# A gather kernel with its query weights loaded once: new release times for the gather buffers, a longer lag and a moved work list

## The chip, the cores and the metric

The kernel runs on one core of a Trainium2 chip. The metric is the device time of one execution in microseconds, lower is better. It was timed three times before the change; the profile is one further execution. A run of this kernel repeats within a few microseconds.

## The reference, cut to what matters

One layer of an encoder on 512 tokens of width 1024, all in float32. A modulated LayerNorm, one input projection, two kinds of attention (8 neighbourhood heads, 4 differential heads), an output projection and a second LayerNorm come first. The second half, which takes most of the time, is a retrieval over 16384 experts, each with one down row and one up row of 1024 numbers:

```python
qc = (xc @ w_query).reshape(CHUNK, HEADS, 2, DKEY // 2)          # 8 heads
s_half = einsum('chpk,pnk->chpn', qc, sub_keys)                  # 2 x 128 key scores
top_s, top_i = top_k(s_half, 16)                                 # then top 16 of the 16 x 16 sums
expert, g = ..., softmax(best_s)
act = gelu(einsum('chkd,cd->chk', expert_down[expert], xc))
out = einsum('chkd,chk->cd', expert_up[expert], g * act)
```

The output is a LayerNorm of the residual and this sum.

## The kernel before, in words

The 512 tokens are 4 tiles of 128. A **head** is here one token tile with one retrieval head: 32 heads, in the order (tiles 0 and 1, retrieval heads 0 to 3), (tiles 0 and 1, 4 to 7), then tiles 2 and 3 likewise. Each head chooses 16 experts for each of its 128 tokens. A **set** is one of these 16 choices: 512 sets. For every set GpSimd issues two indirect DMAs (L623), each of 128 rows of 4 KB: the **down gather** and the **up gather**.

- The down gather is reduced by VectorE: one instruction multiplies it with the tokens and sums the row (L1379, "the dot").
- After four dots ScalarE takes the Gelu (L889), VectorE multiplies in the softmax weight (L1336, `weigh`), ScalarE spreads four weights on diagonal matrices (L1026), and TensorE adds weight times up gather to the tile's sum (L837).
- A gathered block lies in a **place** until its dot or its matmuls are done. `PLACES` is 8. Places are given out in the order of the gathers, the one used longest ago first; a gather waits for the last use of its place. `LATE_PLACES` adds four places each time a weight buffer has been used for the last time: by query weights of chunk 0 for tile 1 (new places from about set 62 of the down gathers), chunk 1 for tiles 2 and 3 (269), and chunk 2 (305). `PLACE_SETS` is how many sets after that use the places may be asked for.
- `gather_order` writes out the order of the 1024 gathers on GpSimd's queue: down gather `at`, then up gather `at - UP_LAG` (7). Gathers are counted here from 0 in this order; set 0's up gather is gather 8.

The retrieval starts before the first half has ended. `FIRST_GROUPS` are TensorE's pieces of work (groups) before the first up matmul. What is left of it is listed in `SCHEDULE` as (first slot, pieces per slot, groups): after the up matmuls of set `at` TensorE does the pieces of slot `at`. A group is an output projection half (`out`, 8 pieces, L691), a transposition (`mix_t` L681, `u_t` L673), 128 query columns (`query`, 8 pieces, L665), or key scores (L699). Each group writes a PSUM bank; `bank_at` gives it, and `wait_for_bank` lets the first piece wait until the group before in the same bank has been read. Groups in `FIRST_GROUPS` use bank `(g + 3) % 6` after the attention, groups behind them bank `4 + g % 2`.

ScalarE reads query, key score and transposition groups (`evacuate`), in line with its diagonals: a group ended at slot s is read after the diagonal of set s + `EVAC_AFTER` (3). VectorE reads `out` groups in `add_mix`, after the dot named by `ADD_AT`. After the dots named by `LN_FROM` it does eight steps of LayerNorm of token tile 1, 2 and 3; steps 2 and 6 wait for a square root on ScalarE (`ln_deviation`, L875). In the first 8 sets of each head it also chooses the experts of the head after it (`choose`, two steps per set). `residual` (L1347 and on) and `finish` close a token tile after head 12 (tile 0), 16, 28 and at the end.

SyncE loads weights. The 512 columns of query chunk 0 and chunk 1 are loaded during the first half, chunk 2 and 3 over the buffers of the output projection after its last use. In the kernel before, chunk 1's buffer is given to places 8 to 11, and chunk 1 is loaded a second time (2 MB, into chunk 0's buffer) after chunk 0's last use.

Of the kernel before, what the change touches and what calls it, by code (L numbers as in the profile page):

```python
# [72 lines left out]
LATE_PLACES = [(0, ("query", (1, 3, 1, 1))), (1, ("query", (1, 3, 2, 2))), (2, ("query", (2, 3, 2, 2)))]  # L73
PLACE_SETS = 16
QUARTER = 4
UP_LAG = QUARTER + 3
FIRST_UP = UP_LAG
# [21 lines left out]
def query_slot(c, first):  # L99

    return QUERY_SLOT[0] if c == 1 and first >= 2 else QUERY_SLOT[c]


# [11 lines left out]
CHOOSE_FIRST = {31 + i: (i // 8, 2 * (i % 8)) for i in range(16)}  # L115


def phase_a_groups():
# [9 lines left out]
    for a in range(len(ATT) + 3):  # L128
# [4 lines left out]
        if a >= 3:  # L133
# [3 lines left out]
    g += [("query", (1, b, 0, 1)) for b in range(4)] + [("key_scores", (1, 0))]  # L137
# [21 lines left out]
EVAC_AFTER = 3
# [108 lines left out]
def build(nc, x, c, w_ada, b_ada, w_in, w_out, na_rpb, t5_bias, lambda_q1, lambda_k1, lambda_q2,  # L268
# [3 lines left out]
    with ctx:  # L272
# [180 lines left out]
        def _(sp):  # L453
# [75 lines left out]
            def load_query(c, slot, last_use):  # L529

                sp.wait_ge(pe_group, INDEX[last_use] + 1)
                sp.dma_start(w_slot[slot], w_query[0, :, c * HALF:(c + 1) * HALF]
                             .rearrange("(k p) n -> p k n", p=P)).then_inc(w_in_slot[slot], 16)

            load_query(2, QUERY_SLOT[2], ("out", (TILES - 1, 0)))
            load_query(3, QUERY_SLOT[3], ("out", (TILES - 1, 1)))
# [3 lines left out]
            load_query(1, query_slot(1, 2), ("query", (0, 3, 2, 2)))  # L540
# [88 lines left out]
        def _(pe):  # L629
# [31 lines left out]
            def query_part(ps, c, b, first, n, k):  # L661
# [3 lines left out]
                return nc.tensor.matmul(ps[:, 0:n * P], w_slot[query_slot(c, first)][:, k, b * P:(b + 1) * P],  # L665
# [197 lines left out]
        def _(act):  # L863
# [155 lines left out]
            def diagonals(head, q):  # L1019

                act.wait_ge(weight_done, head * QUARTER + q + 1)
                for j in range(q * QUARTER, (q + 1) * QUARTER):
# [5 lines left out]
                    for group in ended_at(at - EVAC_AFTER):  # L1028
# [443 lines left out]
```

## Time and profile before

| | us |
|---|---|
| median of 3 runs | 1754.54 (1750.51 to 1756.98) |
| profiled execution, its own time | 1758.13 |
| its span, first to last instruction | 1756.3 |
| TensorE, VectorE, ScalarE, GpSimd busy | 1479.7, 1140.1, 432.3, 985.6 |
| DMA traffic | 606.02 MB, mean 345 GB/s |

Busy time is a sum over very different stages. The span has two: the first half up to about 380 us, bound by the engines, and the gathers after it. The rows of the slices and windows show how fast data moved in each; a slice is 43.9 us.

### The profile page before, as it was taken

What the parts mean: (1) busy time and instruction counts of PE and PEld (TensorE: products, weight loads), DVE (VectorE), ACT (ScalarE), POOL (GpSimd) and SP (SyncE); (2) the same over time, 40 slices, a digit from 0 to 9 for tenths busy, and PEclk for the clock granted to TensorE, in tenths of its full rate; (3) what the DMA queues carried; (4) which work ended last, traced back from release to release, by engine and by line L of the source; (5) the groups of instructions that cost most, each with busy time, mean ns of one, the idle gap of its engine ahead of it and who ended that gap; (6) DMA issues with size and microseconds to landing.
All of it is one profiled execution on the core that took longest, in us unless ns stands there. A gap on an engine that the chain in (4) does not pass through costs nothing.

```text
span 1756.3 us, 14526 instructions
## 1 busy us (share of the span) xinstructions
PE 1479.7 (84%) x4096; PEld 684.0 (39%) x4096; DVE 1140.1 (65%) x2797; ACT 432.3 (25%) x1096; POOL 985.6 (56%) x1055
## 2 busy tenths in 40 slices
PE   5999989879899989977798799987899777777776
PEld 5444455654454345422343344432344222222222
DVE  6543055777867657776767666776666766677753
ACT  2111142441322222222222222322222222222221
POOL 1000000036767757777776677777777777777771
PEclk9899997989999999999999999999999999999999
DMA  9869221069999999999999999999999999999993
GB/s 308 326 224 218 96 72 21 7 242 374 390 388 409 406 366 391 409 409 409 409 409 408 408 409 409 410 410 409 410 409 409 409 409 409 410 409 409 410 409 152
DMA packets 190679, 606.02 MB, mean 345 GB/s; under 512 B 30704, under 2 KB 31112, under 8 KB 190440
## 3 DMA queue, kind: packets, MB, share of 16 engines
q0 software_dynamic: 147456, 536.94, 77.1%
q1 hardware_dynamic: 41799, 64.29, 11.3%
q10 hardware_dynamic: 1344, 3.87, 0.8%
q8 instruction: 34, 0.56, 0.1%
q14 instruction: 46, 0.37, 0.1%
HBM read 601.68 MB, written 3.34 MB: 344 GB/s over the span
## 4 chain that ended last, share of the span: by engine, by line
DMA 40%; PE 27%; POOL 14%; DVE 11%; issue 7%; ACT 1%; SPq 0%; DVEq 0%; POOLq 0%; ACTq 0%
DMA big<-in_expert_down,expert_idx 14%; DMA big<-in_expert_up,expert_idx 13%; PE pair L633 12%; POOL big L623 11%; PE pair L837 9%; DMA region_v<-in_expert_down,expert_idx 6%; DMA region_v<-in_expert_up,expert_idx 6%; POOL region_v L623 3%; PE pair L691 3%; DVE big L1379 3%; DVE big L1212 1%; DMA big<-in_w_ada 1%; PE pair L665 1%; PE pair L785 1%; DVE region_v L1379 1%
## 5 line engine op out<-in xcount | busy, mean ns | idle before, releaser
L837 PE MATMUL pair<-big 128*128 128x512 f32 x1460 | 710.1, 610 | 159.7 <-DMA big<-in_expert_up,expert_idx 147.0
L1379 DVE CUSTOM_DVE_ANT_0 big<-big,pair 128x1024 f32<-128x1024 f32 x363 | 442.6, 1220 | 250.1 <-DMA big<-in_expert_down,expert_idx 245.7
L837 PEld LDWEIGHTS pair<-big 128*128 128x128 f32 x1460 | 252.0, 190 | 547.3 <-issue 502.7
L623 POOL DMA_INDIRECT big<-in_expert_down,expert_idx x363 | 344.3, 948 | 150.1 <-issue 91.8
L623 POOL DMA_INDIRECT big<-in_expert_up,expert_idx x365 | 348.4, 955 | 127.1 <-issue 79.5
L837 PE MATMUL pair<-region_v,big 128*128 128x512 f32 x588 | 284.2, 606 | 61.6 <-DMA region_v<-in_expert_up,expert_idx 58.6
L1379 DVE CUSTOM_DVE_ANT_0 region_v<-region_v,pair 128x1024 f32<-128x1024 f32 x149 | 181.5, 1220 | 100.3 <-DMA region_v<-in_expert_down,expert_idx 97.7
L1026 ACT ACTIVATE big<-ident,big 128x128 f32<-128x128 f32 x512 | 167.1, 391 | 311.2 <-DVE big L1336 311.2
L633 PE MATMUL pair<-big 128*128 128x512 f32 (+1 forms) x480 | 194.2, 599 | 0.0
L837 PEld LDWEIGHTS pair<-region_v,big 128*128 128x128 f32 x588 | 101.8, 190 | 208.1 <-issue 187.9
L582 POOL TENSOR_SCALAR small<-small 128x4 f32<-128x4 f32 (+1 forms) x6 | 1.4, 236 | 318.6 <-DVE small L1308 282.1
L623 POOL DMA_INDIRECT region_v<-in_expert_down,expert_idx x149 | 141.3, 948 | 62.9 <-issue 38.3
L623 POOL DMA_INDIRECT region_v<-in_expert_up,expert_idx x147 | 139.4, 948 | 55.3 <-issue 30.2
L889 ACT ACTIVATE big<-big 128x4 f32<-128x4 f32 x128 | 26.1, 204 | 505.5 <-DVE big L1379 505.5
L665 PE MATMUL pair<-big 128*128 128x256 f32 (+1 forms) x640 | 141.2, 338 | 0.8 <-ACT big L925 0.8
L665 PEld LDWEIGHTS pair<-big 128*128 128x128 f32 x640 | 104.6, 191 | 86.7 <-issue 85.1
L633 PEld LDWEIGHTS pair<-big 128*128 128x128 f32 (+1 forms) x480 | 84.3, 196 | 93.3 <-issue 91.7
L925 ACT ACTIVATE big<-pair 128x512 f32<-128x512 f32 (+2 forms) x74 | 33.5, 457 | 214.0 <-PE pair L665 107.8
L691 PE MATMUL pair<-big 128*128 128x512 f32 x128 | 65.0, 620 | 0.7 <-issue 0.7
L1212 DVE SCALAR_TENSOR_TENSOR big<-big,small 128x512 f32<-128x512 f32 x84 | 63.2, 752 | 3.0
L1003 ACT ACTIVATE big<-pair 128x512 f32<-128x512 f32 (+3 forms) x70 | 37.6, 540 | 109.9 <-PE pair L633 99.7
L944 ACT ACTIVATE big<-big,small 128x256 f32<-128x256 f32 (+1 forms) x64 | 39.1, 610 | 78.3 <-DVE small L1284 78.3
(148 smaller groups left out, 1029.4 us busy)
## 6 DMA issues: line engine op xcount, KB each, us to landing
big<-in_w_ada SPq DMA_DIRECT2D x12, 2048.0 KB, 18.2
big<-in_w_in SPq DMA_DIRECT2D x6, 2048.0 KB, 17.0
big<-in_w_query SPq DMA_DIRECT2D x5, 2048.0 KB, 18.9
big<-in_expert_up,expert_idx POOLq DMA_INDIRECT x365, 15.5
big<-in_expert_down,expert_idx POOLq DMA_INDIRECT x363, 15.3
big<-in_w_out SPq DMA_DIRECT2D x2, 2048.0 KB, 10.3
big<-na_scr SPq DMA_DIRECT2D x24, 128.0 KB, 5.0
region_v<-in_expert_down,expert_idx POOLq DMA_INDIRECT x149, 13.0
```

The lines of the kernel that those rows point to most:

```text
L623: nc.gpsimd.indirect_dma_start(places[place], None, (expert_down if kind == "down" else expert_up)[0], bass.IndirectOffsetOnAxis(expert_id ...
L633: last = nc.tensor.matmul(ps, a, b, start=(i == 0), stop=(i == len(pairs) - 1))
L665: return nc.tensor.matmul(ps[:, 0:n * P], w_slot[query_slot(c, first)][:, k, b * P:(b + 1) * P], src, start=(k == 0), stop=(k == KB - 1))
L691: return nc.tensor.matmul(ps[:, :], src, w_slot[OUT_SLOT[s]][:, k, :], start=(k == 0), stop=(k == KB - 1))
L837: last = nc.tensor.matmul(pair[t % 2][:, s * HALF:(s + 1) * HALF], diag[:, j, :], places[place][:, s * HALF:(s + 1) * HALF], start=(h == 0 ...
L889: nc.scalar.activation(acts[:, head % 2, lo:lo + QUARTER], at_head(dots, head)[:, lo:lo + QUARTER], ACT.Gelu).then_inc(gelu_done, 1)
L925: nc.scalar.activation(dst, ps, ACT.Copy).then_inc(act_evac, 1)
L944: nc.scalar.activation(exps, raw, ACT.Exp, bias=row_min[:, slot:slot + 1], scale=-1.0, accum_out=row_sum[:, slot:slot + 1]).then_inc(exp_d ...
L1003: nc.scalar.activation(dst, ps, ACT.Copy, scale=scale).then_inc(act_evac, 1)
L1026: nc.scalar.activation(diag[:, j, :], ident[:, :], ACT.Copy, scale=weights[:, head % 2, j:j + 1]).then_inc(diag_done, 1)
L1212: last = v.scalar_tensor_tensor(out=acc, in0=w[:, k, :], scalar=c_exp[:, k:k + 1], in1=acc, op0=ALU.mult, op1=ALU.add)
L1379: v.tensor_tensor_reduce(out=places[place], in0=places[place], in1=u_cur[:, :], scale=1.0, scalar=0.0, op0=ALU.mult, op1=ALU.add, accum_ou ...
```

## The change

Chunk 1 is loaded once: `query_slot` goes, and the second load on SyncE's queue with it. Chunk 1's buffer is therefore busy until slot 245, and the first four late places come from chunk 0's buffer instead. With `PLACE_SETS` 20 the places are 8 until down set 229, 12 until 265, 16 until 301 and 20 from there. The lag between down and up gathers is 10 for sets below 140 and 7 from there (at sets 140 to 142 two up gathers follow each down gather). Group reads on ScalarE move to s + lag - 2. `out (1, 0)` moves from slots 0 to 7 into `FIRST_GROUPS`, as group 229 of what are now 230, and most of the schedule moves ahead by some slots. LayerNorm of tiles 1, 2 and 3 starts at sets 24, 142 and 152, where it started at 25, 92 and 168.

```diff
 PLACES = 8
-LATE_PLACES = [(0, ("query", (1, 3, 1, 1))), (1, ("query", (1, 3, 2, 2))), (2, ("query", (2, 3, 2, 2)))]
-PLACE_SETS = 16
+LATE_PLACES = [(1, ("query", (0, 3, 2, 2))), (0, ("query", (1, 3, 2, 2))), (2, ("query", (2, 3, 2, 2)))]
+PLACE_SETS = 20
-FIRST_UP = UP_LAG
+LONG_LAG, LONG_UNTIL = 10, 140
...
-CHOOSE_FIRST = {31 + i: (i // 8, 2 * (i % 8)) for i in range(16)}
+CHOOSE_FIRST = {32 + i: (i // 8, 2 * (i % 8)) for i in range(16)}
...
-    g += [("query", (1, b, 0, 1)) for b in range(4)] + [("key_scores", (1, 0))]
+    g += [("query", (1, b, 0, 1)) for b in range(4)] + [("key_scores", (1, 0)), ("out", (1, 0))]
...
-SCHEDULE = [(0, 1, [("out", (1, s)) for s in range(2)]), (18, 1, [("mix_t", (2, s)) for s in range(2)]),
-            (26, 4, [("u_t", (1, s)) for s in range(2)]),
-            (28, 4, [("query", (0, b, 1, 1)) for b in range(4)]), (38, 1, [("key_scores", (0, 1))]),
-            (39, 4, [("query", (1, b, 1, 1)) for b in range(4)]), (49, 1, [("key_scores", (1, 1))]),
-            (50, 2, [("out", (2, s)) for s in range(2)]),
-            (60, 1, [("mix_t", (3, 0))]), (63, 1, [("mix_t", (3, 1))]), (66, 1, [("out", (3, s)) for s in range(2)]),
-            (85, 2, [("query", (2, b, 0, 2)) for b in range(4)]), (103, 1, [("key_scores", (2, t)) for t in range(2)]),
-            (105, 2, [("query", (3, b, 0, 2)) for b in range(4)]), (123, 1, [("key_scores", (3, t)) for t in range(2)]),
+SCHEDULE = [(0, 1, [("out", (1, 1))]), (20, 1, [("mix_t", (2, s)) for s in range(2)]),
+            (22, 4, [("u_t", (1, s)) for s in range(2)]),
+            (24, 4, [("query", (0, b, 1, 1)) for b in range(4)]), (34, 1, [("key_scores", (0, 1))]),
+            (35, 4, [("query", (1, b, 1, 1)) for b in range(4)]), (45, 1, [("key_scores", (1, 1))]),
+            (46, 2, [("out", (2, s)) for s in range(2)]),
+            (56, 1, [("mix_t", (3, 0))]), (59, 1, [("mix_t", (3, 1))]), (62, 1, [("out", (3, s)) for s in range(2)]),
+            (80, 2, [("query", (2, b, 0, 2)) for b in range(4)]), (98, 1, [("key_scores", (2, t)) for t in range(2)]),
+            (100, 1, [("query", (3, b, 0, 2)) for b in range(4)]), (133, 1, [("key_scores", (3, t)) for t in range(2)]),
...
-LN_FROM = {1: 25, 2: 92, 3: 168}
-ADD_AT = {15: (1, 0), 23: (1, 1), 62: (2, 0), 67: (2, 1), 82: (3, 0), 90: (3, 1)}
+LN_FROM = {1: 24, 2: 142, 3: 152}
+ADD_AT = {14: (1, 0), 23: (1, 1), 63: (2, 0), 68: (2, 1), 84: (3, 0), 92: (3, 1)}
-WEIGHED = [max(QUARTER * (n + 1), 2 * QUARTER) for n in range(HEADS * QUARTER - 1)]
+WEIGHED = [max(QUARTER * (n + 1), LONG_LAG + n) for n in range(HEADS * QUARTER - 1)]
...
+def lag_at(at):
+    return LONG_LAG if at < LONG_UNTIL else UP_LAG
+
+def evacuated_at(at):
+    return [g for slot in range(max(0, at - LONG_LAG), at + 1) if slot + lag_at(slot) - 2 == at
+            for g in ended_at(slot)]
...
-            if at >= FIRST_UP and ups <= at - UP_LAG:
+            if ups <= at - lag_at(at):
...
-            load_query(1, query_slot(1, 2), ("query", (0, 3, 2, 2)))
...
-                    for group in ended_at(at - EVAC_AFTER):
+                    for group in evacuated_at(at):
```

## Rows read from the trace of the kernel before

**Rows 1.** The page's slices of 43.9 us: data moved, GB/s.
```profile
GB/s 308 326 224 218 96 72 21 7 242 374 390 388 409 406 366 391 409 409 409 409 409 408 408 409 409 410 410 409 410 409 409 409 409 409 410 409 409 410 409 152
```

**Rows 2.** Windows: span, busy us of each engine, PE clock, DMA share, GB/s.
```profile
380.00:412.00 32.00, 27.84 (x108) 16.25 (x107) 18.32 (x39) 10.20 (x25) 20.98 (x24) 0.89 0.92 334
...
440.00:460.00 20.00, 16.11 (x40) 6.42 (x40) 16.20 (x32) 11.18 (x22) 14.81 (x15) 1.00 0.98 370
460.00:500.00 40.00, 36.25 (x147) 20.76 (x147) 27.62 (x67) 7.85 (x25) 29.68 (x33) 1.00 1.02 408
500.00:520.00 20.00, 19.10 (x87) 11.90 (x85) 15.24 (x47) 6.82 (x18) 12.30 (x14) 1.00 0.97 360
...
640.00:680.00 40.00, 34.94 (x103) 18.99 (x103) 34.41 (x80) 13.15 (x31) 25.80 (x26) 1.00 0.93 345
680.00:960.00 280.00, 237.51 (x605) 103.94 (x604) 205.33 (x506) 74.78 (x188) 205.98 (x218) 1.00 1.03 409
```

**Rows 3.** The page's DMA parts: the gathers' queue, and the query loads.
```profile
q0 software_dynamic: 147456, 536.94, 77.1%
...
big<-in_w_query SPq DMA_DIRECT2D x5, 2048.0 KB, 18.9
```

**Rows 4.** Timeline of GpSimd: start, us, instruction, idle before and releaser.
```profile
382.97 1.09 POOL L623 DMA_INDIRECT big<-in_expert_up,expert_idx  x1 [0.19 <-issue]
...
397.21 0.93 POOL L623 DMA_INDIRECT big<-in_expert_down,expert_idx  x1 [0.30 <-DVE big L1379]
...
479.20 0.94 POOL L623 DMA_INDIRECT region_v<-in_expert_down,expert_idx  x1 [0.30 <-issue]
```

**Rows 5.** Timeline of VectorE: dots of sets 12, 14, 16, 24 and 43.
```profile
402.44 1.22 DVE L1379 CUSTOM_DVE_ANT_0 big<-big,pair 128x1024 f32<-128x1024 f32 x1 [2.85 <-DMA big<-in_expert_down,expert_idx]
...
409.78 1.22 DVE L1379 CUSTOM_DVE_ANT_0 region_v<-region_v,pair 128x1024 f32<-128x1024 f32 x1 [1.63 <-DMA region_v<-in_expert_down,expert_idx]
...
417.37 1.22 DVE L1379 CUSTOM_DVE_ANT_0 big<-big,pair 128x1024 f32<-128x1024 f32 x1
...
437.91 1.22 DVE L1379 CUSTOM_DVE_ANT_0 big<-big,pair 128x1024 f32<-128x1024 f32 x1
...
486.92 1.22 DVE L1379 CUSTOM_DVE_ANT_0 region_v<-region_v,pair 128x1024 f32<-128x1024 f32 x1 [1.33 <-DMA region_v<-in_expert_down,expert_idx]
```

**Rows 6.** Timeline of VectorE: its three long waits for ScalarE, and a LayerNorm step.
```profile
447.75 0.16 DVE L1085 RECIPROCAL small<-small 128x1 f32<-128x1 f32 x1 [2.57 <-ACT small L875]
...
505.51 0.22 DVE L1336 SCALAR_TENSOR_TENSOR big<-big 128x4 f32<-128x4 f32 x1 [4.11 <-ACT big L889]
...
642.39 0.16 DVE L1085 RECIPROCAL small<-small 128x1 f32<-128x1 f32 x1 [10.51 <-ACT small L875]
642.59 1.28 DVE L1086 SCALAR_TENSOR_TENSOR x_sb<-x_sb,small,big 128x1024 f32<-128x1024 f32 x1
```

**Rows 7.** Timeline of TensorE: key scores, first up matmuls, output projection pieces.
```profile
387.11 1.13 PE L699 MATMUL pair<-keys_t,big 128*128 128x128 f32 x8 [0.46 <-ACT big L925]
391.94 3.75 PE L837 MATMUL pair<-big 128*128 128x512 f32 x4 [3.71 <-ACT big L1026]
395.49 1.92 PE L691 MATMUL pair<-big 128*128 128x512 f32 x2
...
528.18 1.88 PE L691 MATMUL pair<-big 128*128 128x512 f32 x4
...
531.61 1.88 PE L691 MATMUL pair<-big 128*128 128x512 f32 x4
```

**Rows 8.** Timeline of VectorE: head scaling, the first `add_mix` read, `residual`.
```profile
410.93 0.87 DVE L1119 TENSOR_SCALAR big<-big,small 128x128 f32<-128x128 f32 x4
...
415.92 0.69 DVE L1106 TENSOR_TENSOR big<-pair,mods 128x512 f32<-128x512 f32 x1 [2.23 <-PE pair L691]
...
932.48 1.28 DVE L1347 TENSOR_TENSOR big<-pair,mods 128x512 f32<-128x512 f32 x2
...
936.51 1.17 DVE L1379 CUSTOM_DVE_ANT_0 region_v<-region_v,pair 128x1024 f32<-128x1024 f32 x1
```

More of the change, by code:

```diff
@@ L96, in key_blocks @@
     return WINDOW // P if ATT[a][1] < NA_HEADS else SEQ // P
-def query_slot(c, first):
-    return QUERY_SLOT[0] if c == 1 and first >= 2 else QUERY_SLOT[c]
 def octet_runs(t):
@@ L153 @@
             (172, 1, [("u_t", (t, s)) for t in (2, 3) for s in range(2)]),
             (178, 1, [("query", (0, b, 2, 2)) for b in range(4)]), (212, 1, [("key_scores", (0, t)) for t in (2, 3)]),
-            (222, 1, [("query", (1, b, 2, 2)) for b in range(4)]), (256, 1, [("key_scores", (1, t)) for t in (2, 3)]),
-            (258, 1, [("query", (2, b, 2, 2)) for b in range(4)]),
-            (292, 1, [("key_scores", (2, 2))]), (324, 1, [("key_scores", (2, 3))]),
+            (214, 1, [("query", (1, b, 2, 2)) for b in range(4)]), (248, 1, [("key_scores", (1, t)) for t in (2, 3)]),
@@ L158 @@
+            (250, 1, [("query", (2, b, 2, 2)) for b in range(4)]),
+            (284, 1, [("key_scores", (2, 2))]), (324, 1, [("key_scores", (2, 3))]),
             (326, 1, [("query", (3, b, 2, 2)) for b in range(4)]), (360, 1, [("key_scores", (3, t)) for t in (2, 3)])]
-EVAC_AFTER = 3
 SCALE_AT = 14
-LN_FROM = {1: 25, 2: 92, 3: 168}
-ADD_AT = {15: (1, 0), 23: (1, 1), 62: (2, 0), 67: (2, 1), 82: (3, 0), 90: (3, 1)}
+LN_FROM = {1: 24, 2: 142, 3: 152}
+ADD_AT = {14: (1, 0), 23: (1, 1), 63: (2, 0), 68: (2, 1), 84: (3, 0), 92: (3, 1)}
@@ L527, in _, with load_query @@
                 sp.dma_start(ln1_rows[:, i, :], v[0].partition_broadcast(P)).then_inc(ln1_in, 16)
-            def load_query(c, slot, last_use):
+            def load_query(c, last_use):
                 sp.wait_ge(pe_group, INDEX[last_use] + 1)
[L532 to L536, printed above, removed]
+                sp.dma_start(w_slot[QUERY_SLOT[c]], w_query[0, :, c * HALF:(c + 1) * HALF]
+                             .rearrange("(k p) n -> p k n", p=P)).then_inc(w_in_slot[QUERY_SLOT[c]], 16)
+            load_query(2, ("out", (TILES - 1, 0)))
+            load_query(3, ("out", (TILES - 1, 1)))
             sp.wait_ge(u_ready, TILES)
@@ L652, in query_weights @@
             def query_weights(c, first, n):
-                slot = query_slot(c, first)
-                loads = 2 if c >= 2 or slot != QUERY_SLOT[c] else 1
+                loads = 1 if c < 2 else 2
+                slot = QUERY_SLOT[c]
                 pe.wait_ge(w_in_slot[slot], 16 * (STREAM_LOADS[slot] + loads))
@@ L664, in query_part @@
                 src = u_t[:, k, lo:lo + n * P] if (c, first) != (0, 0) else qk_t[:, k + 4 * (k // 4), P:2 * P]
-                return nc.tensor.matmul(ps[:, 0:n * P], w_slot[query_slot(c, first)][:, k, b * P:(b + 1) * P],
+                return nc.tensor.matmul(ps[:, 0:n * P], w_slot[QUERY_SLOT[c]][:, k, b * P:(b + 1) * P],
                                         src, start=(k == 0), stop=(k == KB - 1))
```

## The prediction

> **What bounds the kernel now.** I read the page's slices first. From the eleventh slice on data moves at 366 to 410 GB/s, and at 408 to 410 from the eighteenth to the last but one [rows 1]: the second half of the kernel is bound by the DMA engines at 409 GB/s, and what counts there is bytes, plus the time in which the DMA engines run dry. The windows show where they do: 380 to 412 us at 334 GB/s, 440 to 460 at 370, 500 to 520 at 360, 640 to 680 at 345 [rows 2]. In time that is (409-334)/409 x 32 = 5.9 us, then 1.9, 2.4 and 6.3 us, 16.5 in all. The stretch 680 to 960 moves 409, and nothing is lost there. So I count two things: bytes removed, and dry time removed or added. A gather is 536.94 MB / 1024 = 0.524 MB [rows 3], or 1.28 us at 409 GB/s, and a set (two gathers) 2.56 us.
>
> Then the timelines of the engines at the dry places. Two of them follow a wait of VectorE for ScalarE: 2.57 us at 447.75 (the square root of LayerNorm 1), 4.11 us at 505.51 (a Gelu), and so does the third, 10.51 us at 642.39 (square root, LayerNorm 2) [rows 6]. While VectorE waits no dot is done, no place comes free, and GpSimd can't issue. ScalarE was late because it reads a TensorE group three sets after its slot, while up gathers are seven behind: it stands until TensorE gets there, and Gelu and square root stand behind it in its order.
>
> **How much eight places cover.** With eight places a place is wanted again after 8 x 1.28 = 10.3 us. The gather issued at 397.21 into a nearly empty queue was used at 402.44, 5.2 us; the one issued at 479.20 into a full one at 486.92, 7.7 us [rows 4, 5]. At 7.7 the engines saturate (408 GB/s from 460 to 500, with eight places [rows 2]), and I take 5.2 as the point where they run dry. An up gather's place also needs 1.9 us of matmuls and 0.4 of issue, so TensorE may be late by 10.3 - 5.2 - 2.3 = 2.8 us before time is lost; a dot takes 1.22 plus 0.3, so VectorE may be late by 3.5 us. GpSimd issues every 0.94 + 0.30 = 1.24 us [rows 4] against 1.28 for the transfer, so cover once used comes back at only 0.04 us a gather. That is what the change gives up: from set 62 to 229 it has eight places where there were twelve.
>
> The Trainium skill ("DMA: Bandwidth & Descriptors", Anatomy of one DMA) gives one such DMA a fixed 2.0 us beside its bytes, so some 3.2 us for a gather as an estimate. This trace has 5.2 as its short case and does not bear that out; by the page's figure every cover would be 2.0 us larger, the three losses of cover reckoned below 2.1, 0.5 and 0 instead of 4.1, 2.5 and 0.5, and the sum -7.1 instead of -2.6 us.
>
> **The change part by part.**
>
> *The second load of chunk 1* goes: 2.10 MB [rows 3] at 409 GB/s, in a saturated stretch: -5.1 us. It can't be hidden there, since anything else would move instead; the lower end is -5.1, the upper 0.
>
> *Later reads on ScalarE and the lag of ten.* A read now comes lag - 2 sets behind its slot: 8 for lag 10, 5 for lag 7, against 3 for lag 7. That is two sets (5.1 us) more for TensorE, more than the 4.11 us by which VectorE stood at 505.51. The three waits go: the dry time at 440, 500 and 640 is -1.9, -2.4 and -6.3 us. LayerNorm's square roots now also fall on quarters (24, 142, 152) whose diagonals have no group in front. The extra gathers at sets 140 to 142 are only order. Upper end of this part: 0.
>
> *`out (1, 0)` before the first up matmul.* TensorE ends its key scores at 388.2 and stands 3.71 us [rows 7]; eight pieces of two matmuls at 0.43 (the four at 528.18 and the next four pieces' start at 531.61 are 3.43 apart with eight matmuls in between [rows 7]) are 6.9 us, to 395.1, and the first up takes until 396.8. So far it is nearly free. But now the first group of the schedule, `out (1, 1)`, meets a full bank. `out (1, 0)` is group 229, bank (229 + 3) % 6 = 4; `out (1, 1)` is group 230, bank 4 + 230 % 2 = 4. It waits until `add_mix(1, 0)` has read the bank, behind the dot of set 14 on VectorE. When is that? The first eleven gathers are now downs, then they alternate, so down 14 is gather 18. Gather 8 goes out at 382.97 [rows 4], ten more at 1.24 bring 395.4; landing after 5.2 to 6, dot 1.22, four scalings 0.87, a product of the size of the read, 0.69, and the read itself, 0.69 [rows 8]: 404.9. TensorE stands from 396.8 to 404.9.
>
> Behind it: up matmul 1. Gather 21 (up 5) takes the place of up 1 and stops GpSimd's queue, downs too. After its 3.71 us of idle TensorE ran at half clock: four up matmuls 3.75 us against 1.88, two pieces' matmuls 1.92 [rows 7]. I take the same here: 404.9 + 1.7 + 3.5 + 0.4 = 410.5 for the issue, landing at 415.7. In the kernel before gather 21 is down 14, used at 409.78 [rows 5]. The landing line moves 5.9 us back: +6.0 us. The time is not won back, for after it transfers are saturated. Bounds: 0 (if the queue in front hid it) and +9.
>
> The Trainium skill ("TensorE: Matmul & The Clock Gate", Why this matters for your kernels) says to leave no idle gaps between bursts, as the clock falls to half. The rows agree (PE clock 0.89 over 380 to 412 [rows 2]); without it this term would be 2.6 us smaller.
>
> *`out (2, ...)` at slots 46 to 53* takes two pieces a slot: TensorE 3.43 us per set [rows 7] against 2.56 for the data, 8 x 0.87 = 6.9 us late. Before, it stood at slots 50 to 57, and the twelve places came just then (up set 54 is the first in a new place). Now there are eight: 6.9 - 2.8 = +4.1 us. Bounds 0 and 6.9. The other slots have at most 0.86 us of pieces beside 1.71 of ups, which is 2.57: no loss, no gain. `query (3, ...)` at one piece a slot relieves TensorE where nothing was lost.
>
> *LayerNorm 2 at sets 142 to 149* meets the selection of head 10. A dot with its selection steps takes (437.91 - 417.37 - 1.4) / 8 = 2.39 us [rows 5]; six sets are 14.3, LayerNorm's long steps 1.28 each [rows 6], some 5.6 in those sets, and `choose` of head 10 waits about 1.5 for the key scores read after the diagonal of 141. 21.4 against 15.4: 6.0 late, less 3.5: +2.5 us. Bounds 0 and 6. LayerNorm 1 and 3 lie in sets without selection, 2.5 us a set, free.
>
> *`residual` of tile 0* at set 208 takes 936.51 - 932.48 = 4.0 us [rows 8], hidden by twelve places then, by 3.5 now: +0.5. Bounds 0 and 4.
>
> *Two selection steps one attention step later* (`CHOOSE_FIRST`): the same instructions, 0 (from -1 to +1). Places from set 230 on (12, 16, 20) are within four sets of before; the end is unchanged: 0.
>
> Sum: -5.1 - 1.9 - 2.4 - 6.3 + 6.0 + 4.1 + 2.5 + 0.5 = -2.6 us on the profiled 1758.1. The median of the runs shown is 3.6 below that: 1754.5 - 2.6 = 1752.
>
> **The rivals.**
>
> *A, the cover holds after the start.* The pieces at 46 to 53, LayerNorm 2 and `residual` cost nothing. For it: 460 to 500 us was saturated with eight places [rows 2]. Then -15.7 + 6.0 = -9.7: 1744.8.
>
> *B, the bank wait is hidden too.* For it: the data queued at 397 still flow for some microseconds. Against: GpSimd has nothing more in flight than eight. -15.7: 1738.8.
>
> *C, slower: eight places don't carry sets 62 to 229.* The ordinary bursts of VectorE at the start of each head (copy of the tokens, selection, LayerNorm, `add_mix`), 1.3 us each, run the queue dry each time, since it is refilled at 0.04 us a gather. It decides from where the cover is under 1.3 us, which means a latency of about 7.4 in place of 5.2. For it: the wait of 2.57 at 447.75 already cost 1.9 us. Against: the window of A. Ten heads at 1.3 are +13: 1765.
>
> *D, the load was no cost.* If the gathers lose their share elsewhere, 5.1 come back: 1757.
>
> **How the numbers follow.** The forecast 0.52, A 0.18, B 0.05, C 0.20, D 0.05. A measurement of this kernel can tell 0.5%, 8.8 us, from no change. Faster by more (under 1745.8): most of A, all of B, 0.20. Slower by more (over 1763.3): most of C, 0.16. The rest 0.64. The range takes in A and nearly all of C: 1743 to 1764.
>
> **What would show it.** TensorE standing some 8 us before its second up matmul, released by VectorE, half clock behind it, and GpSimd standing at gather 21. No Gelu or square root wait over 2 us on VectorE. Data under 409 GB/s at four places only: 400 to 416, about 525 to 550 (slots 46 to 53), LayerNorm 2, and hardly at set 208; 409 elsewhere, and 2.1 MB less in all. Wrong if windows between sets 62 and 229 fall short of 409 throughout (C), or if GpSimd runs through gather 21 (B).

## The result, and the profile after

| | before | changed |
|---|---|---|
| median us (range, runs) | 1754.43 (1750.51 to 1756.98, 6) | 1760.98 (1758.52 to 1763.09, 6) |
| profiled execution, its own time | 1758.13 | 1763.09 |
| its span | 1756.3 | 1761.3 |
| DMA traffic, MB | 606.02 | 603.92 |

The ratio is 1.004, 95% interval 1.0027 to 1.0052: slower by about 7 us, where 2.6 us faster was forecast. The time is inside the range given (1743 to 1764); the sign was wrong.

The slices and the loads on the page of the changed kernel. They answer to [rows 1] and [rows 3]:

```profile
GB/s 307 326 223 211 101 72 24 2 233 306 409 409 352 406 406 408 409 381 381 409 409 396 410 410 409 409 410 409 409 409 409 409 409 409 409 409 409 410 409 174
...
L695 PE MATMUL pair<-big 128*128 128x512 f32 x128 | 64.0, 621 | 10.2 <-DVE big L1110 9.4
...
big<-in_w_query SPq DMA_DIRECT2D x4, 2048.0 KB, 13.7
```

One weight load less. The slices under 409 are now the tenth (306), the thirteenth (352), the 18th and 19th (381) and the 22nd (396): the four places that the prediction named, and no others. The `out` matmuls have a wait of 9.4 us on `add_mix` in their group.

The windows of the changed kernel (stretch, length; busy us and count of PE, PEld, DVE, ACT, POOL; PE clock, DMA share, GB/s). They answer to [rows 2]:

```profile
380.00:412.00 32.00, 21.21 (x97) 13.68 (x98) 23.55 (x45) 11.04 (x28) 16.50 (x18) 0.84 0.80 303
412.00:440.00 28.00, 26.31 (x60) 10.78 (x58) 16.09 (x48) 2.77 (x9) 19.93 (x22) 1.00 0.89 336
440.00:460.00 20.00, 15.20 (x32) 5.56 (x33) 18.82 (x36) 10.28 (x19) 15.06 (x16) 1.00 1.03 409
...
500.00:520.00 20.00, 20.00 (x94) 12.71 (x93) 15.16 (x48) 5.77 (x18) 14.47 (x16) 1.00 1.03 409
520.00:560.00 40.00, 39.27 (x100) 17.65 (x99) 26.92 (x61) 8.01 (x21) 25.11 (x27) 1.00 0.96 355
560.00:640.00 80.00, 67.36 (x160) 28.03 (x159) 49.27 (x117) 14.88 (x42) 52.51 (x57) 1.00 1.02 402
640.00:680.00 40.00, 38.93 (x120) 21.46 (x119) 27.36 (x70) 10.22 (x28) 28.75 (x31) 1.00 1.03 409
...
760.00:800.00 40.00, 31.51 (x84) 13.73 (x83) 30.85 (x72) 11.83 (x23) 25.79 (x27) 1.00 0.96 358
800.00:840.00 40.00, 28.30 (x57) 9.92 (x56) 33.43 (x80) 13.25 (x29) 29.39 (x31) 0.96 1.02 398
920.00:960.00 40.00, 37.32 (x95) 16.57 (x95) 30.25 (x74) 12.32 (x29) 28.39 (x31) 1.00 1.01 395
1100.00:1720.00 620.00, 491.36 (x1093) 185.67 (x1092) 428.90 (x1049) 142.52 (x377) 458.74 (x483) 1.00 1.03 409
```

Dry time is (409 - rate)/409 times the width:

| place | before | forecast | measured |
|---|---|---|---|
| start, 380 to 440 | 5.9 | 11.9 | 8.3 + 5.0 = 13.3 |
| three waits of VectorE on ScalarE (440, 500, 640) | 10.6 | 0 | 0 |
| `out (2, ...)`, 520 to 640 | 0 | 4.1 | 5.3 + 1.4 = 6.7 |
| LayerNorm 2, 760 to 840 | 0 | 2.5 | 5.0 + 1.1 = 6.1 |
| `residual`, 920 to 960 | 0 | 0.5 | 1.4 |
| sum | 16.5 | 19.0 | 27.5 |

With the bytes: -5.1 - 16.5 + 27.5 = +5.9 us; the profiled executions differ by +5.0, the medians by +6.5. So the sum was made of the right terms. Those that were added came out too small by 8.5 us together: the three terms of cover by 7.1 (14.2 in place of 7.1), the bank wait by 1.4. The last of the stretches above moves 409, as before: nothing is lost from set 230 on.

The bank wait, in the timelines of TensorE, GpSimd and VectorE of the changed kernel (start, length, engine, line, operation, in brackets the idle time in front and who ended it):

```profile
396.57 1.88 PE L841 MATMUL pair<-big 128*128 128x512 f32 x4
407.89 2.07 PE L695 MATMUL pair<-big 128*128 128x512 f32 x2 [9.44 <-DVE big L1110]
409.75 3.03 PE L841 MATMUL pair<-region_v,big 128*128 128x512 f32 x4
412.62 1.02 PE L695 MATMUL pair<-big 128*128 128x512 f32 x2
```

```profile
400.35 0.94 POOL L627 DMA_INDIRECT region_v<-in_expert_down,expert_idx  x1 [0.30 <-issue]
413.05 0.94 POOL L627 DMA_INDIRECT region_v<-in_expert_up,expert_idx  x1 [11.76 <-PE pair L841]
```

```profile
404.49 1.22 DVE L1383 CUSTOM_DVE_ANT_0 big<-big,pair 128x1024 f32<-128x1024 f32 x1 [1.33 <-DMA big<-in_expert_down,expert_idx]
...
405.63 0.87 DVE L1123 TENSOR_SCALAR big<-big,small 128x128 f32<-128x128 f32 x4
406.54 0.69 DVE L1126 TENSOR_TENSOR big<-big,subln 128x512 f32<-128x512 f32 x1
407.15 0.68 DVE L1110 TENSOR_TENSOR big<-pair,mods 128x512 f32<-128x512 f32 x1
```

This is the chain of the prediction link by link: dot 14, four scalings, the product, the read of the bank, then TensorE (after 9.44 us of idling, at half the clock: 2.07 us for two matmuls against 1.02 further on), then gather 21, the up gather at 413.05. GpSimd stands for 11.76 us with no gather issued. What data do meanwhile, in 5 us windows:

```profile
400.00:405.00 5.00, 0.00 (x0) 0.00 (x0) 2.47 (x6) 4.15 (x8) 0.99 (x2) 0.68 1.03 416
405.00:410.00 5.00, 2.11 (x3) 1.08 (x4) 4.71 (x11) 0.15 (x1) 0.00 (x0) 0.50 0.18 69
410.00:415.00 5.00, 5.00 (x10) 2.10 (x10) 0.00 (x0) 0.06 (x1) 1.64 (x2) 0.80 0.10 11
415.00:420.00 5.00, 5.00 (x13) 2.18 (x12) 0.51 (x1) 0.00 (x0) 3.60 (x5) 1.00 0.93 324
```

### The profile page after: what moved, and what is told of

It is laid out like the page before. It is cut to its first block, busy times and chain, and to the rows that moved or that the text cites. A ratio compares the mean times of both kernels' runs of the same rounds, so it can differ in the third digit from the quotient of the medians.

```text
span 1761.3 us, 14525 instructions
## 1 busy us (share of the span) xinstructions
PE 1482.9 (84%) x4096; PEld 679.7 (39%) x4096; DVE 1140.1 (65%) x2797; ACT 432.2 (25%) x1096; POOL 985.6 (56%) x1055
## 2 busy tenths in 40 slices
DMA packets 189638, 603.92 MB, mean 343 GB/s; under 512 B 30687, under 2 KB 31095, under 8 KB 189399
## 4 chain that ended last, share of the span: by engine, by line
DMA 37%; PE 27%; POOL 16%; DVE 10%; issue 8%; ACT 1%; SPq 0%; DVEq 0%; POOLq 0%; ACTq 0%
DMA big<-in_expert_down,expert_idx 12%; PE pair L637 12%; POOL big L627 11%; DMA big<-in_expert_up,expert_idx 10%; PE pair L841 9%; DMA region_v<-in_expert_up,expert_idx 9%; DMA region_v<-in_expert_down,expert_idx 6%; POOL region_v L627 5%; PE pair L695 3%; DVE big L1383 2%; PE pair L669 1%; DVE big L1216 1%; DVE region_v L1383 1%; DMA big<-in_w_ada 1%; PE pair L789 1%
## 5 line engine op out<-in xcount | busy, mean ns | idle before, releaser
L841 PE MATMUL pair<-big 128*128 128x512 f32 x1344 | 653.2, 609 | 139.1 <-DMA big<-in_expert_up,expert_idx 137.2
L1383 DVE CUSTOM_DVE_ANT_0 big<-big,pair 128x1024 f32<-128x1024 f32 x336 | 409.8, 1220 | 244.6 <-DMA big<-in_expert_down,expert_idx 240.2
L841 PEld LDWEIGHTS pair<-big 128*128 128x128 f32 x1344 | 230.4, 189 | 496.9 <-issue 464.1
L841 PE MATMUL pair<-region_v,big 128*128 128x512 f32 x704 | 342.2, 609 | 71.9 <-DMA region_v<-in_expert_up,expert_idx 67.1
L627 POOL DMA_INDIRECT big<-in_expert_down,expert_idx x336 | 320.4, 953 | 139.5 <-issue 88.5
L627 POOL DMA_INDIRECT big<-in_expert_up,expert_idx x336 | 318.6, 948 | 117.1 <-issue 75.2
L1383 DVE CUSTOM_DVE_ANT_0 region_v<-region_v,pair 128x1024 f32<-128x1024 f32 x176 | 214.5, 1220 | 148.9 <-DMA region_v<-in_expert_down,expert_idx 147.4
L841 PEld LDWEIGHTS pair<-region_v,big 128*128 128x128 f32 x704 | 121.4, 190 | 248.7 <-issue 226.6
L627 POOL DMA_INDIRECT region_v<-in_expert_up,expert_idx x176 | 167.8, 953 | 81.4 <-PE pair L841 50.0
L627 POOL DMA_INDIRECT region_v<-in_expert_down,expert_idx x176 | 166.3, 945 | 62.9 <-issue 46.3
L669 PEld LDWEIGHTS pair<-big 128*128 128x128 f32 x640 | 104.5, 191 | 93.8 <-issue 92.0
L695 PE MATMUL pair<-big 128*128 128x512 f32 x128 | 64.0, 621 | 10.2 <-DVE big L1110 9.4
```

The lines of the kernel that those rows point to most:

```text
L627: nc.gpsimd.indirect_dma_start(places[place], None, (expert_down if kind == "down" else expert_up)[0], bass.IndirectOffsetOnAxis(expert_id ...
L669: return nc.tensor.matmul(ps[:, 0:n * P], w_slot[QUERY_SLOT[c]][:, k, b * P:(b + 1) * P], src, start=(k == 0), stop=(k == KB - 1))
L695: return nc.tensor.matmul(ps[:, :], src, w_slot[OUT_SLOT[s]][:, k, :], start=(k == 0), stop=(k == KB - 1))
L841: last = nc.tensor.matmul(pair[t % 2][:, s * HALF:(s + 1) * HALF], diag[:, j, :], places[place][:, s * HALF:(s + 1) * HALF], start=(h == 0 ...
L1383: v.tensor_tensor_reduce(out=places[place], in0=places[place], in1=u_cur[:, :], scale=1.0, scalar=0.0, op0=ALU.mult, op1=ALU.add, accum_ou ...
```

## The experiments

The runs were made on several chips, and the pace of the gathers differs between them; whether it is the chip itself or what else ran on it is not on record. The comparison above and the first four experiments had 409 GB/s. All later runs were made on four other chips. There the late stretch, 1100 to 1720 us with up to 20 places, moves 363 to 369 GB/s, below "365" for short, and the kernel before takes 1869 to 1883 us. Ratios are to the kernel before on the same chip.

**At 409 GB/s (kernel before 1753.2 us): each suspected term alone.** All four start from the changed kernel.

Bank of the second output group:

```diff
-        return 4 + g % 2
+        return 4 + (g + 1) % 2
```

> The changed kernel with the two banks behind the first groups swapped, so that out (1, 1) meets an empty bank. Theory: the wait of TensorE for add_mix (9.44 us) and the one of GpSimd at gather 21 (11.76 us) go, the dry time of 380 to 440 us falls from 13.3 to about 6 us, and the time from 1761.0 by 7 to about 1754. Rival: the data in flight hid the wait and the dry time belongs to the start of the gathers; then less than 2 us.

Selection steps of the first heads at their old place:

```diff
-CHOOSE_FIRST = {32 + i: (i // 8, 2 * (i % 8)) for i in range(16)}
+CHOOSE_FIRST = {31 + i: (i // 8, 2 * (i % 8)) for i in range(16)}
```

> The changed kernel with the two selection steps of each attention step back where they were (CHOOSE_FIRST 31). Theory: the last two steps, 1.8 us on VectorE, no longer stand ahead of the last map's difference; gather 4 goes out at 376.5 instead of 378.8 and the kernel ends 2.3 us earlier, at 1758.7. Rival: the later start was chance or is won back in the wait for the bank: 0.

`out (2, ...)` at one piece a slot:

```diff
-            (46, 2, [("out", (2, s)) for s in range(2)]),
-            (56, 1, [("mix_t", (3, 0))]), (59, 1, [("mix_t", (3, 1))]), (62, 1, [("out", (3, s)) for s in range(2)]),
+            (43, 1, [("out", (2, s)) for s in range(2)]),
+            (59, 1, [("mix_t", (3, 0))]), (62, 1, [("mix_t", (3, 1))]), (63, 1, [("out", (3, s)) for s in range(2)]),
...
-ADD_AT = {..., 68: (2, 1), ...}
+ADD_AT = {..., 70: (2, 1), ...}
```

> The changed kernel with out (2, 0) and out (2, 1) at one piece a slot (slots 43 to 58) instead of two (46 to 53); mix_t of tile 3 and out (3) follow within three slots. Theory: eight places cover hardly any lateness (under 1 us), so all 6.2 us of dry time between 530 and 565 us go: 1755. Rival, as I had predicted: the cover of TensorE is 2.8 us, 4.1 us go and the dry time has another part: 1757.

LayerNorm 2 in front of the selection of head 10:

```diff
-LN_FROM = {1: 24, 2: 142, 3: 152}
+LN_FROM = {1: 24, 2: 136, 3: 152}
```

> The changed kernel with LayerNorm 2 at sets 136 to 143, which have no selection, instead of 142 to 149. Theory, with hardly any cover: the dry time of 760 to 805 us (6.0 us) goes nearly whole, 1756. Rival, cover of 3.5 us for VectorE: 2.5 us, 1758.5.

| | ratio to before (95% interval) | median us | against the changed kernel (1.004) |
|---|---|---|---|
| bank | 0.9985 (0.9975 to 0.9996) | 1750.39 | -9.6 us |
| selection steps | 1.0028 (1.0016 to 1.004) | 1758.71 | -2.1 us |
| `out (2, ...)` | 1.0013 (1.0003 to 1.0022) | 1755.23 | -4.7 us |
| LayerNorm 2 | 1.0014 (1.0005 to 1.0024) | 1755.34 | -4.6 us |

The last column is the difference of two ratios times 1753.2, each known to about 0.1%, so some 3 us either way: the selection steps aren't told from nothing, the other three are. The trace with the selection steps at their old place says that they may be worth more than 2.1: there gather 4 goes out at 371.50 us, where the traces of the changed kernel and of the other three edits have 378.2 to 378.8. That is 7 us earlier, where 2.3 were expected. The edits for the bank, `out (2, ...)` and LayerNorm 2 mend their own stretch each; here are the windows with the bank mended, then with `out (2, ...)`, then with LayerNorm 2 (those of the changed kernel for the same stretches are 319, 358 and 367 GB/s):

```profile
380.00:440.00 60.00, 54.38 (x175) 26.97 (x176) 50.09 (x114) 17.68 (x45) 44.98 (x48) 1.00 1.01 396
520.00:570.00 50.00, 46.73 (x114) 20.42 (x113) 34.00 (x79) 10.09 (x27) 32.85 (x35) 1.00 0.97 359
```

```profile
520.00:570.00 50.00, 48.63 (x123) 21.84 (x122) 38.31 (x90) 11.03 (x30) 36.06 (x39) 1.00 1.00 392
```

```profile
520.00:570.00 50.00, 46.76 (x120) 21.13 (x120) 35.48 (x84) 10.57 (x28) 32.74 (x34) 1.00 0.98 361
755.00:815.00 60.00, 49.34 (x122) 20.25 (x121) 48.70 (x110) 21.54 (x47) 43.73 (x45) 1.00 1.01 396
```

From 319 to 396 GB/s over 60 us is (396 - 319)/409 x 60 = 11.3 us for the bank. With the bank mended the start runs at 396, where the kernel before had 370 over the same 60 us:

```profile
380.00:440.00 60.00, 55.69 (x172) 28.25 (x170) 42.99 (x102) 14.06 (x38) 41.30 (x46) 0.94 0.97 370
```

This gain comes with `out (1, 0)` in `FIRST_GROUPS` and the lag of ten together; no run parts them. For the other two, from 358 to 392 over 50 us is 4.2 us, and from 367 to 396 over 60 us is 4.3. So the bank conflict alone outweighs what the change lost; the changed kernel with its bank mended is the fastest version measured at 409 GB/s.

**How few places carry the gathers.** The changed kernel with seven places, and with six, timed once each; then seven again on two more chips.

```diff
-PLACES = 8
+PLACES = 7
```

> The changed kernel with seven places in place of eight, to measure how much eight cover. Look at stretches with one piece a slot or none, such as sets 32 to 44 and 152 to 200. Theory: a gather takes some 7.3 us from issue to landing when the queue only just stays full, so a place is used for 7.3 + 2.3 us, and seven places give 7 x 0.524 MB in 9.6 us = 382 GB/s. Rival, the 5.2 us of my prediction: 7.5 us per round of seven, less than the 9.0 us of the transfers, so still 409 GB/s.

> The changed kernel with six places. Theory: 6 x 0.524 MB in 9.6 us = 328 GB/s in the same stretches. Rival with 5.2 us: 7.5 us per round against 7.7 us of transfers, 409 GB/s still, or just under.

> The changed kernel with seven places once more: the last time all transfers, also the late ones with 20 places, moved at some 365 GB/s, which seven places could keep up with. At 409 GB/s in the late stretch: theory (7.3 us from issue to landing where the queue just stays full) 382 GB/s at sets 152 to 200; rival (5.2 us) 409 GB/s.

> The changed kernel with seven places. If the late stretch moves at 409 GB/s: theory 382 GB/s at sets 152 to 200 (7.3 us from issue to landing where the queue just stays full), rival 409 GB/s (5.2 us).

Seven gave 1894.29, 1892.04 and 1899.47 us beside 1876.48, 1877.43 and 1882.71 of the kernel before (0.8 to 0.9% over), six 1909.36. These were chips of 365 GB/s, where a gather takes 0.524/365 = 1.44 us, so they can't give the dry point at 409. What they do say, in one and the same stretch with six places, with seven, and with eight (the changed kernel, the last run below):

```profile
700.00:960.00 260.00, 197.18 (x486) 82.84 (x484) 165.13 (x392) 64.69 (x156) 167.73 (x175) 0.99 0.96 356
```

```profile
700.00:960.00 260.00, 202.44 (x490) 85.61 (x491) 171.69 (x416) 63.76 (x154) 168.87 (x177) 0.97 0.98 363
```

```profile
700.00:960.00 260.00, 203.86 (x494) 84.56 (x494) 177.44 (x430) 61.10 (x152) 174.15 (x183) 0.99 0.98 368
```

The other two runs with seven places have 360 and 361. So each place still counts, at this pace too. Six places at 356 GB/s are 1.47 us a gather and turn around in 8.8 us; less 2.3 us of matmuls and issue, 6.5 are left from issue to landing, as a mean over a stretch that has the ordinary bursts of VectorE in it. With 5.2 (my figure) they would have turned around in 7.5 us and carried 368 easily. With the 7.3 of the expectation they would have carried 328, so that was too much. The estimate goes by one trace each, six and seven places on one chip, eight on another; on the chips of the other two runs with seven places the changed kernel with all four mends (below) has 369 and 365.

**The load of chunk 1 alone.** The kernel before, without its second load; the columns of chunk 1 for tiles 2 and 3 are multiplied with the weights of chunk 0, so it leaves out the right scores there. It gathers as many rows, but other ones. Run on three chips.

```diff
-            load_query(1, query_slot(1, 2), ("query", (0, 3, 2, 2)))
...
-                loads = 2 if c >= 2 or slot != QUERY_SLOT[c] else 1
+                loads = 2 if c >= 2 else 1
```

> The kernel before without the second load of query chunk 1 (its columns for tiles 2 and 3 are computed from chunk 0's weights, which lie in that buffer; the work of every engine is the same). Theory: 2.1 MB at 409 GB/s, 5.1 us less than before. Rival: the load was hidden beside the gathers, 0.

> The kernel before without the second load of query chunk 1, once more (chunk 1's columns of tiles 2 and 3 are computed from chunk 0's weights), since 0.9984 with an interval from 0.9966 to 1.0003 told nothing apart. Theory: 5.1 us, a ratio of 0.997 where data moves at 409 GB/s. Rival: hidden, 1.000.

> The kernel before without the second load of query chunk 1 (its columns of tiles 2 and 3 from chunk 0's weights). Theory: where gathers alone move at 409 GB/s a load can only take their place, 5.1 us, 0.997. Rival: hidden as where gathers move at 365 GB/s, 1.000.

The ratios are 0.9984 (0.9966 to 1.0003), 1.0013 (0.9991 to 1.0034) and 1.0007 (0.9991 to 1.0022): no effect at 365 GB/s, so rival D holds there. The reason is in the windows of 1000 to 1060 us on one of these chips: first a kernel that has the load, issued at 994.76 us (the kernel before with `EVAC_AFTER` 5, below), then the one without it.

```profile
1000.00:1060.00 60.00, 48.36 (x120) 21.23 (x118) 36.96 (x87) 14.67 (x37) 40.52 (x44) 0.94 1.03 409
```

```profile
1000.00:1060.00 60.00, 46.44 (x114) 20.61 (x113) 35.12 (x85) 11.53 (x31) 39.16 (x42) 0.93 0.96 365
```

Gathers alone move 365; with a weight load beside them the total is 409: the load rides on what gathers leave. Where gathers alone move 409 nothing is left over. There, in the trace of the kernel before, the load is issued at 958.18 us, and the total is no higher with it:

```profile
960.00:1020.00 60.00, 46.35 (x118) 19.60 (x117) 37.04 (x85) 13.49 (x36) 40.96 (x44) 1.00 1.03 408
```

So there the gathers make room for it, and the books above close with the load at its full 5.1 us. It was never left out alone at 409 GB/s.

**Later reads on ScalarE alone.** The kernel before, one number changed, on three chips:

```diff
-EVAC_AFTER = 3
+EVAC_AFTER = 5
```

> The kernel before with EVAC_AFTER 5 in place of 3 and nothing else. Theory: the three waits of VectorE for ScalarE (2.57, 4.11 and 10.51 us) go, and with them 10 us of dry time at 440, 500 and 640 us: 8 to 10 us faster than before, about 1744. Rival: the waits are not ScalarE's order but up gathers that come late; then they stay, 0.

> The kernel before with EVAC_AFTER 5, once more, to see its dry places in the profile beside the kernel before at 409 GB/s. Theory: windows 440 to 460, 500 to 520 and 640 to 680 back at 400 or more, 8 to 10 us faster than before. Rival: some of the 6.3 us at 640 to 680 is LayerNorm 2's own work on VectorE over the selection of head 6; then 4 to 6 us.

> The kernel before with EVAC_AFTER 5. Theory at 409 GB/s: 8 to 10 us of the 16.5 us of dry time go, 0.995. Rival: part of the dry time at 640 to 680 us is LayerNorm 2's own work, 4 to 6 us, 0.997.

Ratios 0.9939 (0.992 to 0.9958), 0.9938 (0.9914 to 0.9962) and 0.9933 (0.9908 to 0.9958): some 12 us, at 365 GB/s. This is the part of the change that helps, and it needs neither the single load nor eight places. The rival, that the waits would stay, fell: on one chip the kernel without the second load, `EVAC_AFTER` 3, has VectorE wait for ScalarE up to 10.83 us at 658.37 and 23.14 us at 1267.51; with 5 nothing over 1.4 us is left between 380 and 1100 us, and the longest wait is 10.10 us at 1454.34. Such waits are thus more and longer on these chips than at 409 GB/s, and the 12 us are not the 10.6 us of those three places measured alone.

**All four mends together** on the changed kernel:

> The changed kernel with all four repairs at once: empty bank for out (1, 1), CHOOSE_FIRST 31, out (2) at one piece a slot, LayerNorm 2 at set 136. Theory: the terms are places where the same transfer stream runs dry, so they add: against the kernel before +6.9 - 9.5 - 2.2 - 4.7 - 4.6 is -14 us, about 0.992 of it. Rival: a stall removed moves to the next scarce place, as there is little cover: half of the sum, about 0.997.

> The changed kernel with all four repairs. Theory at 409 GB/s: the terms add, -14 us against the kernel before, 0.992. Rival: half of it, 0.996 to 0.997, as where gathers move at 365 GB/s.

0.9966 (0.9949 to 0.9983) and 0.9949 (0.9934 to 0.9965), at 365 GB/s: faster than before, but not faster than `EVAC_AFTER` alone with twelve places and the second load. The sum of the four mends (0.992) fell in both; with the load worth nothing on these chips it could hardly hold. At 409 GB/s, where it was reckoned, the four were never run together.

**The last two.** The kernel before with `EVAC_AFTER` 5 and LayerNorm 2 in sets without selection (its expectation speaks of seven places, but the kernel before has eight to down set 62 and twelve from there); and the changed kernel once more, on a chip of 365 GB/s.

```diff
-EVAC_AFTER = 3
+EVAC_AFTER = 5
...
-LN_FROM = {1: 25, 2: 92, 3: 168}
+LN_FROM = {1: 25, 2: 88, 3: 168}
```

> The kernel before (seven places to set 230, chunk 1 loaded twice) with EVAC_AFTER 5 and with layer norm 2 at sets 88 to 95, where no selection stands. My theory: VectorE's three long waits on ScalarE go by EVAC_AFTER, worth 12 us at the pace of the three chips seen last; layer norm 2 then stops crossing the selection of head 10, and what is left of a dry stretch there goes too, a further 0 to 2 us. So 0.992 to 0.994. Rival: nothing was left there, so no less than EVAC_AFTER 5 alone (0.9938). If this chip moves the gathers at 409 GB/s, the three dry places are worth 1.9 + 2.4 + 6.3 = 10.6 us together at most, 0.994 of 1753.

> The changed kernel unchanged, beside the kernel before on this chip. At 409 GB/s my theory wants 1.004 again. Where the gathers move at 365 GB/s the load of chunk 1 rides beside them at no cost, so its removal gives nothing and the ratio should be worse: 1.005 to 1.009. Rival: at 365 GB/s the gathers take 1.43 us each against 1.24 us of GpSimd's issue, so GpSimd refills the queue faster and the stalls of the eight places are covered in part: 1.004 or less.

The first gave 0.9917 (0.9889 to 0.9945), 1855.25 us: the lowest ratio of all at 365 GB/s, though its interval takes in `EVAC_AFTER` alone, so the extra 0.2% is not shown. The second gave 1.0006 (0.9985 to 1.0026), 1870.55 us: my theory (1.005 or more) fell and the rival holds. Its windows, besides the 368 over 700 to 960 shown above:

```profile
380.00:440.00 60.00, 47.98 (x158) 24.59 (x157) 39.36 (x94) 13.26 (x36) 35.22 (x39) 0.94 0.84 308
520.00:570.00 50.00, 48.28 (x134) 22.50 (x132) 34.43 (x85) 11.58 (x32) 32.52 (x35) 1.00 0.99 364
```

The other kernel of this pair ran on the same chip and serves as a measure. It has 353 over 380 to 440, also 364 over 520 to 570, and this over LayerNorm 2 and `residual` of the changed kernel:

```profile
700.00:960.00 260.00, 208.04 (x511) 90.19 (x509) 174.62 (x422) 61.47 (x157) 173.19 (x183) 0.98 0.98 374
```

So at this pace `out (2, ...)` loses nothing, the start loses (353 - 308)/365 x 60 = 7.4 us, and LayerNorm 2 and `residual` together (374 - 368)/374 x 260 = 4.2 us, where they lost 7.5 at 409 GB/s. Windows of 20 us on these chips scatter from about 310 to 400 GB/s and more, so only the long ones tell much. The losses of cover are smaller once a gather takes 1.43 us instead of 1.28, but not all gone. This fits a cover that is nearly used up at 409 GB/s; it doesn't prove it.

## Why the prediction was wrong, step by step

**The step that failed** is "I take 5.2 as the point where they run dry". It gave TensorE a cover of 2.8 us and VectorE one of 3.5, which were taken off three terms; those terms came to 14.2 us, not 7.1, and this alone turns -2.6 into +4.5. Dots for which VectorE waited show the real point: there the landing is the start of the dot. In the changed kernel the down gathers of sets 19 and 20, GpSimd's issue and VectorE's dot:

```profile
422.02 0.94 POOL L627 DMA_INDIRECT region_v<-in_expert_down,expert_idx  x1 [0.30 <-issue]
...
424.60 0.94 POOL L627 DMA_INDIRECT region_v<-in_expert_down,expert_idx  x1 [0.31 <-issue]
```

```profile
428.60 1.22 DVE L1383 CUSTOM_DVE_ANT_0 region_v<-region_v,pair 128x1024 f32<-128x1024 f32 x1 [0.30 <-DMA region_v<-in_expert_down,expert_idx]
431.15 1.22 DVE L1383 CUSTOM_DVE_ANT_0 region_v<-region_v,pair 128x1024 f32<-128x1024 f32 x1 [0.45 <-DMA region_v<-in_expert_down,expert_idx]
```

The landings are 2.55 us apart, a full pace, at 6.6 and 6.5 us from issue. And two down gathers of the dry stretch of `out (2, ...)`:

```profile
536.89 0.94 POOL L627 DMA_INDIRECT region_v<-in_expert_down,expert_idx  x1 [0.30 <-issue]
...
550.08 0.94 POOL L627 DMA_INDIRECT region_v<-in_expert_down,expert_idx  x1 [0.30 <-issue]
```

```profile
542.78 1.22 DVE L1383 CUSTOM_DVE_ANT_0 region_v<-region_v,pair 128x1024 f32<-128x1024 f32 x1 [1.58 <-DMA region_v<-in_expert_down,expert_idx]
...
552.31 1.22 DVE L1383 CUSTOM_DVE_ANT_0 big<-big,pair 128x1024 f32<-128x1024 f32 x1 [0.94 <-DMA big<-in_expert_down,expert_idx]
555.24 1.22 DVE L1383 CUSTOM_DVE_ANT_0 region_v<-region_v,pair 128x1024 f32<-128x1024 f32 x1 [0.70 <-DMA region_v<-in_expert_down,expert_idx]
```

The second takes 5.2 us from issue, but lands 2.93 us behind the landing before: at 5.2 the engines are well past dry. The first takes 5.9 us and lands 2.81 us behind the one at 539.97, still less than a full pace. A pairing in the kernel before has 6.3 us at a spacing of 2.55 (issue 521.19, dots 524.94 and 527.49). So by these pairs the point lies between 5.9 and 6.3 us. Beside it the queue wasn't full when the late stretch began: gathers of 522 to 528 took 7.0 to 7.1 us to land, not the 7.7 of the stretch at 479 [rows 4, 5]. Of eight places' 10.3 us, 6.3 and 2.3 leave 1.7 for TensorE, not 2.8, and 6.3 and 1.5 leave 2.5 for VectorE, not 3.5; and GpSimd gave up 2.02 us of its own in front of the stretch:

```profile
530.19 0.94 POOL L627 DMA_INDIRECT big<-in_expert_down,expert_idx  x1 [0.30 <-issue]
533.15 0.95 POOL L627 DMA_INDIRECT big<-in_expert_up,expert_idx  x1 [2.02 <-issue]
...
541.97 0.94 POOL L627 DMA_INDIRECT region_v<-in_expert_up,expert_idx  x1 [1.25 <-PE pair L841]
```

The line at 533.15 shows no wait for a place (the profile names no releaser), and what it is stays open.

The trace of before held the evidence against 5.2. With eight places the wait of 2.57 us at 447.75 [rows 6] cost 1.9 us of dry time and the one of 4.11 us at 505.51 cost 2.4, which leaves a cover of 0.7 and of 1.7 us for a wait of VectorE, where I reckoned with 3.5. With twelve places the 10.51 us at 642.39 cost 6.3, a cover of 4.2, and waits of 4.31 us at 688.43 and 4.18 at 730.34, which the prediction doesn't name, cost nothing (409 GB/s there). By my figures twelve places (12 x 1.28 us) would have covered 15.4 - 5.2 - 1.5 = 8.7 us. These are rough readings: at 448.34 and 451.27 GpSimd's own issues took 1.71 and 1.37 us in place of 0.94, so part of the 1.9 us may be theirs, and VectorE's other work adds to its waits. I had put the first row under rival C and let it change a chance instead of the terms.

*`out (2, ...)`*, forecast 6.9 - 2.8 = 4.1, measured 6.7. TensorE is late by 1.25 us at the gather of each set from 541.97 on, as the 3.43 us per set said; with a cover of 0 to 1.7 us the term would have been 5 to 7. One piece a slot gave 4.7 us back.

*LayerNorm 2*, forecast 6.0 - 3.5 = 2.5, measured 6.1. VectorE was later than the 6.0 us reckoned. The dot of set 144 still waited for its gather, the one of set 150 came 22.7 us later, where six sets of data take 15.4:

```profile
771.31 1.22 DVE L1383 CUSTOM_DVE_ANT_0 big<-big,pair 128x1024 f32<-128x1024 f32 x1 [1.09 <-DMA big<-in_expert_down,expert_idx]
...
794.03 1.22 DVE L1383 CUSTOM_DVE_ANT_0 region_v<-region_v,pair 128x1024 f32<-128x1024 f32 x1
```

That is 7.3 us late for 6.1 lost, a cover of some 1.2 us, less than the 2.5 of the corrected sum. Part of it was gone before: GpSimd first waits for TensorE, 1.21 us in front of the up gather at 763.01 and 1.67 at 772.09 where 0.37 to 0.44 are usual, just behind the sets with two up gathers, to which the prediction gave no time. Then it waits for dots (L1383) in front of the gathers at 785.33 and 792.29, 1.40 and 2.29 us. VectorE's wait for the key scores of head 10, put at 1.5, is 1.24 at 773.91. Moving LayerNorm 2 out of the selection gave 4.6 back; how the rest is shared was not measured.

*`residual`*, 0.5 forecast, 1.4 measured: the same cover, the same direction; no run takes it alone.

*The bank conflict*, forecast +6.0, measured +7.4 (13.3 against 5.9 before). The mechanism, the engine that stands, the gather at which GpSimd stops and the half clock were right; the chain ran 3.0 us later than reckoned (407.89 against 404.9), of which 1.3 to 2.3 us may be that the first gathers of this part go out later (370.96 for 369.68 before, 378.77 for 376.49), since two selection steps stand one step later in VectorE's order. I had priced that at 0; taken back it gave 2.1 us, which the times don't tell from 0, though the gathers of its trace go out 7 us earlier.

On the clock: the granted clock is 0.50 in the window 405 to 410, which is 1.2 GHz, after TensorE had no matmul from 398.5 to 407.9, and 1.00, 2.4 GHz, from 415 on. The Trainium skill ("TensorE: Matmul & The Clock Gate", Why this matters for your kernels) says to leave no idle gaps between bursts, and the trace agrees.

*The three waits*, forecast -10.6, all gone: the longest wait of VectorE on ScalarE after 440 us is the 1.24 above, and `EVAC_AFTER` alone is worth 0.6% on the kernel before at 365 GB/s. *The load*, forecast -5.1: consistent with the books at 409 GB/s, where the total stays at 408 with the load; not told from zero on the slower chips. *The end*: unchanged, as said.

Of the rivals, C (1765) and D (1757) were both 4 us from the 1761 measured. C was right in its premise, that cover is far smaller than 2.8 us, but not in its places, for the ordinary bursts at the head starts cost nothing (409 GB/s between the stretches of the table). D fails at 409 GB/s by the total of 408 with the load in it. A fell because the pieces of work cost 14.2 us, B because GpSimd stood for 11.76 us and data flow with it.

The Trainium skill ("DMA: Bandwidth & Descriptors", Anatomy of one DMA) gives one DMA a fixed 2.0 us beside its bytes, by which a gather would take some 3.2 us, an estimate from that page's figures. This would have made the cover larger still. The traces do not agree: the shortest down gather in flight with others takes 5.2 us, and the sum by that figure, -7.1, was further off than mine.

## What to carry to other kernels

Take the cover of a ring of buffers from stalls whose loss can be read in the same trace (waits of 2.57 and 4.11 us that cost 1.9 and 2.4), not from the shortest time of one transfer. Here the queue was refilled at 1.24 us a gather and drained at 1.28, so it had little cover, and a late engine cost most of what it was late. Before moving a group to the front of a list, look whether its bank, chosen by the group's number, meets that of the next group: here one parity cost 9.6 us and made a kernel that is faster than the one before (0.9985) slower (1.004). Split a change into its parts: one number of it, on the kernel before, was worth 0.6% on the slower chips, at least as much there as the whole with all its mends.

## What was not expected of the hardware

The pace of gathers differed from chip to chip: 409 GB/s on one, 363 to 369 on four others in the same late stretch, while a weight load beside them lifted the total to 409 on the slower ones too. Why is open; the chip itself and other work on it are not told apart. It changes what a change is worth: the changed kernel is 0.4% slower at 409 and not told from the kernel before at 365 (1.0006). A likely reason is that a gather of 1.43 us leaves GpSimd's 1.24 us of issue some slack to refill the queue, and one of 1.28 leaves 0.04. A gather into a nearly empty queue landed in 5.2 us, yet by the pairs above the engines were full only where gathers were issued some 6 us or more before they landed.
